# Expert weights in chunks of 2048 and 1536 columns, with transposes in the banks of w3

## What is computed

```python
D_MODEL = 1024; SEQ = 256; D_FF = 7 * D_MODEL // 2      # 3584
N_EXPERTS = 8; TOP_K = 2

def swiglu(x, w1, w3, w2):
    return (jax.nn.silu(x @ w1) * (x @ w3)) @ w2

def moe_ffn(x, w_router, b_router, w1, w3, w2):
    logits = (x @ w_router + b_router).astype(jnp.float32)
    top_v, top_i = lax.top_k(logits, TOP_K)
    top_w = jax.nn.softmax(top_v, axis=-1)
    gate = jnp.sum(jax.nn.one_hot(top_i, N_EXPERTS) * top_w[..., None], axis=-2)
    out = gate[..., 0:1] * swiglu(x, w1[0], w3[0], w2[0])
    for e in range(1, N_EXPERTS):
        out = out + gate[..., e:e + 1] * swiglu(x, w1[e], w3[e], w2[e])
    return out
```

## Time and profile before

| | |
|---|---|
| median of 3 runs | 2609.4 us |
| profiled execution | 2616.57 us |
| its span | 2614.8 us |
| PE busy | 2393.3 us, 92% of the span |
| DVE, ACT, POOL busy | 768.2, 643.7, 584.2 us |
| HBM read | 540.72 MB |
| loads of expert weights | 189 of 2048 KB, median 12.2 us to landing |

### The profile page before, as it was taken

One profiled execution on the slowest core, in us unless ns is written; L12 is line 12 of the kernel. 1 busy time (PEld: TensorE's weight loads), 2 busy tenths in 40 slices (PEclk: granted clock), 3 DMA queues, 4 the chain that ended last, 5 costly groups with the idle time before them and its releaser, 6 DMA issues. The chain is left out here.

```text
span 2614.8 us, 61998 instructions
## 1 busy us (share of the span) xinstructions
PE 2393.3 (92%) x28274; PEld 1509.7 (58%) x28274; DVE 768.2 (29%) x1363; ACT 643.7 (25%) x974; POOL 584.2 (22%) x362
## 2 busy tenths in 40 slices
PE   4999898779999999698798779999999999999995
PEld 3776677547777778487577654444444444444443
DVE  2237765542222222615765430000000000000002
ACT  1243454332222222325455320100000000000001
POOL 4232542323333443234544300000000000000000
PEclk9999799889999999999799889999999999999997
DMA  7542001336435353231001289999999999999981
GB/s 252 193 161 77 3 4 36 99 130 218 161 129 177 113 181 109 65 121 41 6 4 36 66 325 390 402 400 397 398 401 402 399 397 401 398 372 387 404 348 55
DMA packets 205438, 565.77 MB, mean 216 GB/s; under 512 B 7856, under 2 KB 83008, under 8 KB 199552
## 3 DMA queue, kind: packets, MB, share of 16 engines
q1 hardware_dynamic: 193920, 528.63, 53.9%
q10 hardware_dynamic: 10112, 29.02, 3.4%
q0 software_dynamic: 1152, 4.19, 0.4%
HBM read 540.72 MB, written 21.10 MB: 215 GB/s over the span
## 5 line engine op out<-in xcount | busy, mean ns | idle before, releaser
L701 PE MATMUL bank<-arena 128*32 128x512 f32 (+1 forms) x6624 | 803.4, 557 | 5.9 <-issue 4.8
L311 POOL TENSOR_TENSOR w_lo<-arena,w_hi 128x2048 fp32r<-128x2048 f32 x78 | 354.2, 4542 | 627.0 <-ACT w_hi L305 626.9
L704 PE MATMUL bank<-arena 128*32 128x256 f32 (+1 forms) x6624 | 479.3, 361 | 0.0
L704 PEld LDWEIGHTS bank<-arena 128*32 128x32 f32 x6624 | 215.4, 110 | 435.5 <-issue 410.8
L321 PE MATMUL bank<-h_hi,w_hi 128*128 128x512 f32 (+1 forms) x1008 | 392.0, 389 | 48.1 <-DVE h_lo L1225 42.2
L322 PE MATMUL bank<-h_lo,w_hi 128*128 128x512 f32 (+1 forms) x1008 | 377.2, 374 | 0.0
L323 PE MATMUL bank<-h_hi,w_lo 128*128 128x512 f32 (+1 forms) x1008 | 377.0, 374 | 0.0
L701 PEld LDWEIGHTS bank<-arena 128*32 128x32 f32 x6624 | 208.7, 110 | 125.6 <-issue 10.7
L321 PEld LDWEIGHTS bank<-h_hi,w_hi 128*128 128x128 f32 x1008 | 195.2, 194 | 113.5 <-issue 61.9
L514 POOL DMA_INDIRECT arena<-slot_y,arena x4 | 3.8, 951 | 1028.6 <-ACTq L567 1027.7
L640 DVE TENSOR_TENSOR arena<-arena,bank 128x768 f32<-128x768 f32 (+2 forms) x45 | 31.3, 713 | 664.1 <-ACT arena L542 664.1
(11 more groups left out here) (262 smaller groups left out, 2521.5 us busy)
## 6 DMA issues: line engine op xcount, KB each, us to landing
arena<-in_moe_w_dram SPq DMA_DIRECT2D x189, 2048.0 KB, 12.2
arena<-in_w_mod_dram SPq DMA_DIRECT2D x48, 1024.0 KB, 5.0
arena<-in_ffn_w_dram SPq DMA_DIRECT2D x42, 1024.0 KB, 7.0
arena<-in_w_in_dram SPq DMA_DIRECT2D x26, 1024.0 KB, 6.3
arena<-in_w_out_dram SPq DMA_DIRECT2D x8, 1024.0 KB, 9.6
slot_x<-arena ACTq DMA_DIRECT2D x1, 4992.0 KB, 26.3
slot_y<-arena ACTq DMA_DIRECT2D x1, 4992.0 KB, 55.7
x_store<-arena ACTq DMA_DIRECT2D x2, 2048.0 KB, 6.5
```

The lines of the kernel that those rows point to most:

```text
L311: pool.tensor_tensor(lo, slot_view(splits[i][0]), hi, ALU.subtract).then_inc(sem("w_lo"), 1)
L701: mm(bank[b][64 * h + 32 * c:64 * h + 32 * c + 32, 0:n // 2], xa[:, 32 * c:32 * c + 32], w[:, n // 2 * h:n // 2 * (h + 1)], start=first, s ...
L704: ins = mm(bank[b + 1][blk(q), 0:n // 4], xb, w[:, n // 4 * q:n // 4 * (q + 1)], start=first, stop=last)
```

## The change

Chunks become 2048 and 1536 columns, so an item has two. In `tiled` a half of the columns is now wider than one matmul takes, so there is a loop over pieces of up to 512; a result takes three banks: w1 banks 0 to 2, w3 banks 3 to 5. The transposes go to banks 3 to 5 as well, and `hidden` for w3 waits for `m_gt` before it writes there. Units of w1 and w3 are two rows (2048 or 1536 KB); w2's are two rows in chunk 0 (1024 KB) and three in chunk 1 (1536 KB), and 28 units are one item. w2's rows are dealt out to the partitions in turn: a partition holds two or three neighbouring rows of the matrix, so a contiguous piece is 8 or 12 KB; w1's and w3's are 8 and 6 KB. To match that, the transposes take each second or third column of GSM (`block_cols`). GSM and SGM, now 1536 columns each, move into the space of HB, which is free in this stage.

```diff
-    CHUNKS = [(c, min(1024, FF - c)) for c in range(0, FF, 1024)]
+    CHUNKS = [(c, min(2048, FF - c)) for c in range(0, FF, 2048)]
+    W2_ROWS = (2, 3)
...
-        GSM = area(o_m, 768)
-        SGM = area(o_m + 768, 768)
-        GT = area(o_m + 1536, 6, P)
+        GSM = area(o_hb, 1536)
+        SGM = area(o_hb + 1536, 1536)
+        GT = area(o_m, 12, P)
...
-            return MUNIT // (D if kind == "w2" else CHUNKS[s][1])
+            return W2_ROWS[s] if kind == "w2" else MUNIT // CHUNKS[s][1]
...
         def turned(b, s):
 
             n = CHUNKS[s][1] // 512 * 3
-            return ps[:, b:b + 2, :].rearrange("p b (f n) -> p (b f) n", n=P)[:, 0:n], n
+            return ps[:, b:b + 3, :].rearrange("p b (f n) -> p (b f) n", n=P)[:, 0:n], n
+
+        def block_cols(f, s):
+
+            n = W2_ROWS[s]
+            c = P * n * (f // n) + f % n
+            return slice(c, c + n * (P - 1) + 1, n)
...
-                sp.dma_start(moe_slot(j), src.rearrange("(k p) n -> p k n", p=P)) \
+                src = src.rearrange("(p k) n -> p k n" if kind == "w2" else "(k p) n -> p k n", p=P)
+                sp.dma_start(moe_slot(j), src) \
...
-                src, n = turned(4, s)
+                src, n = turned(3, s)
                 act.activation(GT[:, 0:n], src, ACT.Copy).then_inc(sem("m_gt"), 1)
...
-                for h in range(2):
-                    for c in range(2):
-                        mm(bank[b][64 * h + 32 * c:64 * h + 32 * c + 32, 0:n // 2], xa[:, 32 * c:32 * c + 32],
-                           w[:, n // 2 * h:n // 2 * (h + 1)], start=first, stop=last)
+                for c0 in range(0, n // 2, 512):
+                    nc_ = min(512, n // 2 - c0)
+                    for h in range(2):
+                        for c in range(2):
+                            mm(bank[b][64 * h + 32 * c:64 * h + 32 * c + 32, 0:nc_], xa[:, 32 * c:32 * c + 32],
+                               w[:, n // 2 * h + c0:n // 2 * h + c0 + nc_], start=first, stop=last)
+                    b += 1
                 for q in range(4):
-                    ins = mm(bank[b + 1][blk(q), 0:n // 4], xb, w[:, n // 4 * q:n // 4 * (q + 1)], start=first, stop=last)
+                    ins = mm(bank[b][blk(q), 0:n // 4], xb, w[:, n // 4 * q:n // 4 * (q + 1)], start=first, stop=last)
...
                 pe.wait_ge(sem("m_s" if kind == "w1" else "m_g"), NC * i + s + 1)
+                if kind == "w3":
+                    pe.wait_ge(sem("m_gt"), NC * i + s + 1)
...
-                dst, n = turned(4, s)
+                dst, n = turned(3, s)
                 for f in range(n):
-                    ins = nc.tensor.transpose(dst[:, f], GSM[:, f * P:(f + 1) * P], ident)
+                    ins = nc.tensor.transpose(dst[:, f], GSM[:, block_cols(f, s)], ident)
```

More of the change, by code:

```diff
@@ L445, in spans @@
             n = CHUNKS[s][1]
-            if n == 1024:
-                return [(ps[:, b:b + 2, :].rearrange("p b n -> p (b n)")[:, 0:768], slice(0, 768))]
-            return [(bank[b][:, 0:n // 2], slice(0, n // 2)), (bank[b + 1][:, 0:n // 4], slice(n // 2, n // 2 + n // 4))]
+            if n == 2048:
+                return [(ps[:, b:b + 3, :].rearrange("p b n -> p (b n)"), slice(0, 1536))]
+            return [(ps[:, b:b + 2, :].rearrange("p b n -> p (b n)")[:, 0:n // 2], slice(0, n // 2)),
+                    (bank[b + 2][:, 0:n // 4], slice(n // 2, n // 2 + n // 4))]
         def turned(b, s):
             n = CHUNKS[s][1] // 512 * 3
-            return ps[:, b:b + 2, :].rearrange("p b (f n) -> p (b f) n", n=P)[:, 0:n], n
+            return ps[:, b:b + 3, :].rearrange("p b (f n) -> p (b f) n", n=P)[:, 0:n], n
[3 more added lines that the diff above has]
+            return slice(c, c + n * (P - 1) + 1, n)
         def moe_slot(j):
-            return area(o_ring + (j % MRING) * MUNIT, MUNIT).rearrange("p (k n) -> p k n", k=unit_rows(order[j]))
+            return area(o_ring + (j % MRING) * MUNIT, unit_rows(order[j]), D if order[j][0] == "w2" else CHUNKS[order[j][1]][1])
         def moe_sp(sp):
@@ L643, in item @@
                     dve.wait_ge(sem("m_s"), NC * i + s + 1 + 1)
-                    for src, cols in spans(2, s):
+                    for src, cols in spans(3, s):
                         ins = tt(GSM[:, cols], SGM[:, cols], src, ALU.mult)
@@ L716, in hidden @@
                     for r in range(unit_rows(u)):
-                        ins = tiled(0 if kind == "w1" else 2, CHUNKS[s][1], XG[:, k, 0:NS_A], XG[:, k, NS_A:SLOTS],
+                        ins = tiled(0 if kind == "w1" else 3, CHUNKS[s][1], XG[:, k, 0:NS_A], XG[:, k, NS_A:SLOTS],
                                     moe_slot(place[u])[:, r], k == 0, k == KD - 1)
```

## The result

The changed kernel takes 2624.25 us in the median of six runs (2622.22 to 2630.4), the kernel before, run beside it, 2609.68. The ratio is 1.0058, with a 95% interval of 1.0043 to 1.0072: slower by 14.6 us, against 2626 and +16.4 forecast. The profiled execution took 2624.82 us around a span of 2622.7.

What follows compares the result with a forecast made beforehand. PE was taken as the bound, at 112.55 us an item. The terms 3.41 + 2.70 - 2.85 - 1.28 - 0.16 gave +1.82 us an item, +16.4 for nine, so 2626 us; the range was 2616 to 2642, with 83%.

Steps and rivals of the forecast that it cites:

- PE sets the time: Expert stage: PE, at 112.55 us an item, is the bound; DMA keeps up with little to spare, at 398 GB/s.
- The wait at w3: Before w3 of chunk 1, PE waits for ACT's copy of chunk 0's turned rows: break of 3.41 us, replacing 2.85.
- E: The moment when the matmuls of w1 of chunk 1 would give way to the next row; the w3 wait counts from it.
- The item's end: Before w2 of chunk 1, PE waits for a copy of 1152 columns: 2.70 us with the first row, formerly 1.28.
- Matmuls: Rows of 2048 and 1536 columns take 2.575 and 1.935 us, 16 of each an item: -0.16 us.
- Transposes: 21 an item, as 12 and 9 instead of 6, 6, 6 and 3, each 0.131 us after another; strides cost nothing.
- Rival B: Strided transposes cost double: 2636 us if the nine with step three do, 2651 if all 21; chance 11%.
- Rival C: The clock falls while PE stands 1.5 us for a copy: nine falls, +24.8, 2651 us; chance 8%.
- Rival D, F: D: DMA falls behind at 382 GB/s, 2653 us, 5%. F: rows are paced by supply and get faster, 2557 us, 4%.
- What is hidden: Wider Sigmoid, products and copy: products, about 1.8 us on DVE, lie beside 16 rows, 15 us of PE, costing nothing.
- Rival E: The 4.8 us gap at the loop's turn between items 6 and 7 goes away, saving 7.53 us: 2618; chance 8%.
- What I said would show it: Per item: 1.45 us copy, PE's w3 row 1.5 us after the transposes, copy named as releaser; item ends 114.37 us apart.

Runs made afterwards that it cites:

- s1_supply_before: Kernel before without the matmuls of slots 64 to 95, except in each sum's first and last row, so loads set the time: item 112.09 us.
- e4_w2_pieces: Kernel before with only w2's pieces in chunks of 1024 made 8 KB and transposes of every second column: 2613.79 us, ratio 1.0006.
- e6_copy_twice: Changed kernel with each of ACT's copies of turned rows done twice, one after the other: 2666.26 us, ratio 1.0217.
- e1_early_turn: Changed kernel with chunk 0's twelve transposes after the first two w1 rows of chunk 1, ACT copying before its Sigmoid: 2613.15 us, ratio 1.0004.
- e8_before_unrolled: Kernel before with seven of PE's items unrolled instead of six, nothing else: 2604.23 us, ratio 0.9972.
- e2_both_turns: As e1_early_turn, plus chunk 1's nine transposes in the middle of w2 of chunk 0, with a second GT: 2607.86 us, ratio 0.9979.

## Why the prediction was right

The time, the sign and the mechanism came out as forecast: 2624.25 for 2626, item 114.38 for 114.37. By its steps:

- *PE sets the time.* Right, and closer to wrong than I knew: I had read 398 GB/s as what was delivered, with room above; s1_supply_before shows a bound of 400. That larger pieces earn nothing held, for the reason given (e4_w2_pieces): PE waits on no load.
- *The wait at w3.* 3.41 us forecast from one row's start to the next beyond its length; measured 2058.33 - 2052.99 - 1.935 = 3.41. E is 2054.92, the copy starts at E + 1.86 (forecast 1.87) and PE at E + 3.41, of which 0.10 and not 0.06 after the copy. The slow first row, forecast at 0.03, stayed away: the next row starts 1.93 later.
- *The item's end.* 2.67 forecast for the break and 2.70 with the slow first row; measured 2.67 (2097.12 - 2093.16 - 1.29) and 2.70.
- *Matmuls.* Rows of 2048 and 1536 at 2.575 and 1.935 us. They are 2.575 and 1.935 in the mean of the changed kernel's rows (2052.99 less 2051.06 is one).
- *Transposes.* A term that was right by luck, out of two errors. From 0.80 / 6 I took 0.131 us for a contiguous one; it is 0.114 in the mean of twelve, the rest of the 0.80 being the way from the last one to the next row. Rival B then came true in small: step two and step three cost 0.016 us apiece in the mean of a group, 0.3 us an item instead of 1.18. The two cancel. With the first alone put right the item would have been forecast 0.3 us too short, 2.6 us in nine. I had excluded a cost because the gather's 0.095 us seemed to leave room; it didn't.
- *The rule on 16-byte lines.* The Trainium skill (SBUF — State Buffer, Specifications (TRN2)) says that full rate needs two hits a line, which gives step two free and step three slow. The traces don't part the two that way: step two isn't free (0.120 us against 0.109), and step three is no slower than step two (0.116).
- *Rival C.* None of this kernel's waits on copies (nine of 1.59 us, eight of 0.56, one of 1.22) brought the clock down, but its mechanism is real and was near: in e6_copy_twice it fell behind six of nine waits of 3.07 us and one of eight of 1.72 us, at 1.6 to 1.7 us a time and not the 2.76 of the earlier trace rows.
- *Rival D, F.* Loads fell behind nowhere; no row ran under 1.29 us.
- *What is hidden.* Right: a product of 1536 columns took DVE 1.75 us and PE waited for none. The cover is eight rows, not the 16 I wrote; its 15 us are right.
- *Rival E.* The gap stayed, 4.85 for 4.77; the slow clock behind it cost 2.3 instead of 2.8.
- *What I said would show it.* The releaser of the w3 wait isn't named in the waits; I had expected it to be.

## What to carry to other kernels

A bank that serves two purposes puts the engine that empties it on PE's path; before merging banks, find matmuls that don't need the result and put them between the transposes and the next use, as e1_early_turn does, which gave back 1.66 of 1.83 us. Larger chunks need longer copies at a turn, so a cover that was enough for 384 columns isn't for 1152. And when PE and DMA both stand at nine tenths, cut the work of one and measure the other alone: here the two bounds of the kernel before lay 0.4% apart.

## What was not expected of the hardware

- A transpose whose data are taken at a step of two or three float32 takes 0.120 or 0.116 us to the next against 0.109 contiguous, and its group some 0.055 us more once; its weight load takes 209 or 202 ns against 140.
- The turn of PE's loop costs 4.6 to 5.1 us of nothing and 1.6 to 3.0 us of slow clock behind it in the traces where PE sets the time, at 2600 us 0.3%, with a 16 KB instruction packet landing in each of these gaps. Unrolling that turn away took 0.28% off the kernel before (e8_before_unrolled), where the change with both its waits moved out of the way brought 0.21% (e2_both_turns). The intervals of these two overlap; by the item ends it is 7.5 us against 3.5.
- TensorE's clock fell once behind a wait of 1.72 us that followed 2.0 us of transposes (e6_copy_twice), and not behind seven others like it.
- Loads of 1 to 2 MB in pieces of 6 to 12 KB came at 411 GB/s, loads of 2 MB in pieces of 2 and 4 KB at 400 GB/s, one execution of each.
